# First attention layer on features of the unnormed X, factors per token at its outputs, and moved pieces, waits and low halves in both attention layers

## The chip, the cores and the metric

The kernel runs on one core of a Trainium2 chip. The metric is the device time in microseconds (us) of one execution, the median of several runs. Five engines work side by side, each through its own instructions in program order, and meet through semaphores: TensorE (PE in the profile; PEld is its load of weights), VectorE (DVE), ScalarE (ACT), GpSimd (POOL) and SyncE (SP), which issues most DMAs. PE writes into eight PSUM banks, from which ACT and DVE evacuate to SBUF.

## The reference, cut to what matters

X has 512 tokens of width 1024. Two blocks run one after the other. The first ends with a mixture of experts and a norm of the whole block; the second has two layers of attention and FFN.

```
# first block, per layer: x = x + mixer(rms_norm(x, norm_mix_g)); x = x + hierarchical_moe(rms_norm(x, norm_ffn_g))
return rms_norm(x, norm_final_g)
# second block, per layer i
h = rmsnorm(x, ln1_g[i]) @ w_in[i]
(fq, fk, fv, ff, dq, dk, dv, c_q, c_kv, k_r) = jnp.split(h, split_points, axis=-1)
o_fox = fox_group(fq, fk, fv, ff, fgate_b[i])            # bias from cumsum of log_sigmoid(ff + b)
o_diff = diff_group(dq, dk, dv, lq1, lk1, lq2, lk2, diff_norm_g[i], lam_init)   # ends in rmsnorm(o, norm_g)
o_mla = mla_group(c_q, c_kv, k_r, q_norm_g[i], w_uq[i], kv_norm_g[i], w_ukv[i], pos)
x = x + jnp.concatenate([o_fox, o_diff, o_mla], axis=-1) @ w_o[i]
up = causal_dwconv(rmsnorm(x, ln2_g[i]) @ w_up[i], conv_w[i], conv_b[i])
x = x + (silu(up[:F]) * up[F:]) @ w_down[i]
```

A norm is a factor per token times a gain per channel: (x * r[token] * g[channel]) @ W = r[token] * ((x * g[channel]) @ W). Between the two blocks two norms follow one another: `norm_final_g` on X itself, and `ln1_g[0]` on its result.

## The kernel before

**Stages.** In order of time: a first mixer and its experts to about 668 us, a recurrent mixer and its experts to about 1314 us, the middle norm, attention 1 (1320 to 1600), FFN 1 (to 1965), attention 2 (1965 to 2240, the same rows as attention 1, 642.7 us later) and FFN 2. X (four chunks `c` of 128 tokens) stays in SBUF.

**Dense weights.** Every dense product is a sum of three matmuls of reduced-precision operands: high part of the features by high part of the weights, low by high, high by low. A weight arrives by a DMA that SP issues into one of four raw slots, in units of two halves (4 x 128 rows, up to 512 columns). ACT writes the high part of a half (`W.hi`, L275), and DVE or POOL the low part (`W.lo`, L283: a `tensor_tensor` of 128x1024 or 128x512). In `Weights.add` the halves are numbered in program order; even halves have their low part on DVE, odd ones on POOL. There are six split buffers, so a half is split up to six halves ahead of its use. Within an attention layer halves 0 to 3 belong to the product `mla`, 4 to 7 to `dq`, 8 to 11 to `dk`, 12 to 15 to `dv`, 16 to 19 to `fqk`, 20 to 23 to `fv` and 24 to 31 to the output product `atto` (24 to 27 for its first 512 columns, n = 0).

**Features.** The rows of X (after the norm, `XN`) are transposed by PE (L473, `tensor_half`), two chunks of tokens at a time; ACT writes the high part with the gain as a scale (L481), DVE the low part (L491). `tensor_first_product` (L556) starts the first product on the features of chunks 0 and 1 before those of 2 and 3 are there.

**The end of the experts.** `moe` adds the last expert's result to X by pieces (c, n) of 128 tokens and 512 columns: two matmuls (L1553, L1554) into a bank and one addition of DVE (L1776). All four pieces with n = 0 come ahead of those with n = 1. Behind them PE runs 18 matmuls whose result nobody reads (L408, `tensor_busy`), reads a register and branches on whether more slots of experts are needed (not in these runs).

**The middle norm.** `middle_norm` takes the sum of squares of each chunk (ACT L425, an activation with an accumulator, and its read), its root (L432), a reciprocal (DVE L440), and rescales X in place with `norm_final_g` (DVE L2712; the gain lies in raw slot 0, which becomes free for a next weight only when it was read last). The second norm does the same on that X and writes `XN` (DVE L460). Chunks 0 and 1 come first.

**Attention, PE's order.** Products `mla`, `dq`; transposes of the ranks (L529, wait `ckv`); the `up` products (L2161 and L2164, each group evacuated by ACT or DVE); the cumulated sums of the gates (L2170, wait `cum`); two of the four pieces of `dk` (L2132, 24 matmuls each); transposes of q1 and k1 (L529); and then a pipeline of score steps (L2089, `tensor_scores`; L2120, `tensor_values`) with the rest of `dk`, the products `dv`, `fqk` and `fv` between its steps. DVE applies the norm of the differential heads (L2497, 16 instructions of 128x128) while PE computes `fv`; the next things on DVE are low halves 24, 26 and 28, and then the maxima of the `fox` scores (L2386), for which ACT's exponentials (L2265) wait, and PE for those.

Of the kernel before, what the change touches and what calls it, by code (L numbers as in the profile page):

```python
# [11 lines left out]
ALU = mybir.AluOpType  # L12
ACT = mybir.ActivationFunctionType
AX = mybir.AxisListType.X

P = 128
# [20 lines left out]
TURN_BANKS, PIECE_BANK = (4, 5, 6), (7,)  # L37
# [5 lines left out]
    ("conv_b_2", 88), ("q_norm_g_2", 4), ("kv_norm_g_2", 2), ("norm_ffn_g", 16),  # L43
]
# [106 lines left out]
class Rows:  # L151
# [4 lines left out]
    def __init__(self, XN, before, hi, lo, gain):  # L156
        self.XN, self.before, self.hi, self.lo, self.gain = XN, before, hi, lo, gain
        self.H = (lambda k: hi[:, k, :], lambda k: lo[:, k, :])
        self.done = {}

# [11 lines left out]
class Weights:  # L172
# [23 lines left out]
    def add(self, key, parts, split=True, expert=False):  # L196
# [111 lines left out]
def program(nc, A, pack, const, out):  # L308
# [34 lines left out]
    junk = sb("junk", [P, D], BF16)  # L343

# [108 lines left out]

    def norm_of_rows(rows):
# [8 lines left out]
    def tensor_half(rows, half):  # L463

        rows.done[half] = []
        for j in range(KD // 2):
            bank = banks.take(bf)
            rows.done[half].append(len(bf.banks))
            for k in (2 * j, 2 * j + 1):
                for c in (2 * half, 2 * half + 1):  # L470
                    PE.wait_total(xn, rows.before + (c + 1 if c < NT - 1 else NT + k // (KD // 2)))
# [114 lines left out]
    def plan_cols(key, w, c0, n, order=(0, 1)):  # L586
        for u in order:
            W.add(key, [(4, n, w[512 * u:512 * u + 512, c0:c0 + n].rearrange("(k p) n -> p k n", p=P))])

    def plan_out(key, w, order=(0, 1)):  # L590
        for n in range(2):
            plan_cols((key, n), w, 512 * n, 512, order)
# [210 lines left out]
    lsg, lse = sig("log_sigmoid_in"), sig("log_sigmoid_exp")  # L803

# [572 lines left out]
    def moe(layer, last_square, last_norm, next_half, next_norm):  # L1377
# [178 lines left out]
        def tensor():  # L1556
# [64 lines left out]
        ahead = 2 if next_norm else NT  # L1621

        def scalar():
# [37 lines left out]
            scalar_squares(whole, range(ahead))  # L1661
# [124 lines left out]
        def vector():  # L1786
            vector_route()
            for p in range(PAIRS):
# [18 lines left out]
            for c in range(NT):  # L1807
                vector_combine(c, (0,))
            for c in range(NT):
                if next_norm and c == 3:  # L1810
                    vector_norm(next_norm, ((0, 1), (1, 1)))
                vector_combine(c, (1,))
# [36 lines left out]
        with nc.If(nblocks > 0):  # L1849
            with nc.Fori(0, nblocks):  # L1850
# [85 lines left out]
                for c in range(NT):  # L1936
# [9 lines left out]
                    act.wait_ge(s_loop, n[0])  # L1946
                    step(act.activation(junk[:, :], X[:, c, :], ACT.Square, accum_out=SM[:, c:c + 1]))
                    act.wait_ge(s_loop, n[0])
                    step(act.activation(SM[:, c:c + 1], SM[:, c:c + 1], ACT.Sqrt, bias=ONE[:, 2:3], scale=1.0 / D))
                    act.wait_ge(s_loop, n[0])  # L1950
# [892 lines left out]
```

## Time and profile of the kernel before

| what | value |
|---|---|
| time, median of 3 runs | 2614.44 us (2613.68 to 2616.26) |
| the profiled execution's own time | 2616.33 us |
| its span in the profile | 2615.1 us |
| granted TensorE clock, mean | 0.996 |
| PE busy | 2562.8 us, 98% of the span, 13324 matmuls |
| DVE / ACT / POOL busy | 1133.2 / 914.3 / 356.7 us |

The span begins with the first instruction and ends with the last. Starts are in us from the span's start. In a row of the timeline stand the start, the time from the first start to the last end, engine, line, operation, output <- input and count; in brackets the idle time before, and what ended it. The ends of matmuls are modelled, so neighbouring rows of PE overlap by some tenths. In a row by windows each engine has its busy time and, in parentheses, its instructions; behind them stand the granted clock as a share of 2.4 GHz (0.50 is 1.2 GHz), the busy share of the DMA engines and GB/s.

### The profile page before, as it was taken

What the parts mean: (1) busy time and instruction counts of PE and PEld (TensorE: products, weight loads), DVE (VectorE), ACT (ScalarE), POOL (GpSimd) and SP (SyncE); (2) the same over time, 40 slices, a digit from 0 to 9 for tenths busy, and PEclk for the clock granted to TensorE, in tenths of its full rate; (3) what the DMA queues carried; (4) which work ended last, traced back from release to release, by engine and by line L of the source; (5) the groups of instructions that cost most, each with busy time, mean ns of one, the idle gap of its engine ahead of it and who ended that gap; (6) DMA issues with size and microseconds to landing.
All of it is one profiled execution on the core that took longest, in us unless ns stands there. A gap on an engine that the chain in (4) does not pass through costs nothing.

```text
span 2615.1 us, 32699 instructions
## 1 busy us (share of the span) xinstructions
PE 2562.8 (98%) x13324; PEld 1789.3 (68%) x13324; DVE 1133.2 (43%) x1971; ACT 914.3 (35%) x1741; POOL 356.7 (14%) x160
## 2 busy tenths in 40 slices
PE   9999999999999999999989999999999999999999
PEld 7874444444777444445477778888888767888887
DVE  2543233323685233223353453552554344465264
ACT  4431111111484111111164454442345454443233
POOL 2200000000340000000030011231222002222212
PEclk9999999999999999999999999999999999999999
DMA  6248999999325999999921112232232112223222
GB/s 219 83 193 356 421 421 420 421 421 420 113 97 214 412 420 422 421 421 421 407 80 59 55 65 81 97 108 86 65 117 71 62 33 81 75 87 124 78 65 80
DMA packets 133367, 542.23 MB, mean 207 GB/s; under 512 B 13024, under 2 KB 24672, under 8 KB 84064
## 3 DMA queue, kind: packets, MB, share of 16 engines
q1 hardware_dynamic: 129264, 536.94, 52.5%
q10 hardware_dynamic: 3952, 3.17, 0.4%
q8 instruction: 108, 1.77, 0.3%
q14 instruction: 43, 0.35, 0.0%
HBM read 537.98 MB, written 2.10 MB: 207 GB/s over the span
## 4 chain that ended last, share of the span: by engine, by line
PE 91%; DVE 4%; DMA 2%; ACT 2%; issue 1%; POOL 0%; SPq 0%; POOLq 0%; DVEq 0%; ACTq 0%
PE ps L622 21%; PE ps L1516 16%; PE ps L624 15%; PE ps L1538 8%; PE ps L646 5%; PE ps L1492 4%; PE ps L555 4%; PE ps L2132 3%; PE ps L1553 2%; PE ps L1554 2%; DMA w<-in_moe_w_up 2%; PE ps L2089 2%; PE ps L2120 2%; PE ps L556 1%; PE ps L2111 1%
## 5 line engine op out<-in xcount | busy, mean ns | idle before, releaser
L283 POOL TENSOR_TENSOR w<-w,w 128x1024 fp32r<-128x1024 f32 (+2 forms) x136 | 335.2, 2474 | 2206.3 <-ACT w L275 2202.1
L622 PE MATMUL ps<-w,w 128*128 128x512 f32 x2592 | 590.7, 389 | 2.6 <-POOL w L283 2.6
L622 PEld LDWEIGHTS ps<-w,w 128*128 128x128 f32 x2592 | 486.1, 188 | 104.8 <-POOL w L283 3.4
L1516 PE MATMUL ps<-w,w 128*64 128x512 f32 x2048 | 445.4, 592 | 3.5 <-issue 2.0
L624 PE MATMUL ps<-w,w 128*128 128x512 f32 (+1 forms) x1872 | 408.8, 379 | 5.3 <-DVE w L541 3.0
L624 PEld LDWEIGHTS ps<-w,w 128*128 128x128 f32 x1872 | 337.9, 188 | 72.6 <-issue 5.9
L275 ACT ACTIVATE w<-w 128x1024 fp32r<-128x1024 f32 (+2 forms) x260 | 251.5, 999 | 348.9 <-PE ps L624 177.9
L283 DVE TENSOR_TENSOR w<-w,w 128x1024 fp32r<-128x1024 f32 (+2 forms) x124 | 200.8, 1626 | 350.6 <-ACT w L275 348.1
L1516 PEld LDWEIGHTS ps<-w,w 128*64 128x64 f32 x2048 | 149.0, 137 | 293.6 <-issue 293.6
L1538 PE MATMUL ps<-w,w 128*64 128x512 f32 x1024 | 226.8, 595 | 0.8 <-ACT w L1614 0.8
L1764 DVE TENSOR_TENSOR w<-ps,w 128x512 f32<-128x512 f32 x32 | 34.7, 1083 | 388.8 <-PE ps L1516 388.8
L1538 PEld LDWEIGHTS ps<-w,w 128*64 128x64 f32 x1024 | 70.7, 137 | 139.8 <-issue 138.8
L2634 DVE SCALAR_TENSOR_TENSOR w<-ps,PK,w 128x511 f32<-128x511 f32 (+1 forms) x176 | 131.8, 749 | 75.5 <-ACT w L2590 72.4
L1776 DVE TENSOR_TENSOR X<-ps,X 128x512 f32<-128x512 f32 x256 | 159.5, 679 | 1.1
L646 PE MATMUL ps<-w,w 128*128 128x512 f32 x528 | 122.6, 391 | 0.2 <-DVE X L724 0.2
L1492 PEld LDWEIGHTS ps<-w,w 128*128 128x128 f32 x896 | 111.0, 191 | 2.4
L646 PEld LDWEIGHTS ps<-w,w 128*128 128x128 f32 x528 | 98.5, 188 | 20.7 <-issue 0.6
L1492 PE MATMUL ps<-w,w 128*128 128x256 f32 x896 | 111.6, 282 | 0.0
L1553 PE MATMUL ps<-w,w 128*128 128x512 f32 x256 | 109.0, 426 | 0.0
L1658 ACT ACTIVATE w<-ps,w 128x512 fp32r<-128x512 f32 x64 | 44.0, 688 | 180.3 <-PE ps L1538 180.3
L1783 DVE SCALAR_TENSOR_TENSOR w<-ps,w,w 128x512 fp32r<-128x512 f32 x64 | 48.0, 751 | 133.8 <-ACT w L1658 133.8
L2132 PE MATMUL ps<-w,w 128*128 128x512 f32 x384 | 101.6, 411 | 0.0
(257 smaller groups left out, 2471.4 us busy)
## 6 DMA issues: line engine op xcount, KB each, us to landing
w<-in_moe_w_gate SPq DMA_DIRECT2D x128, 1024.0 KB, 15.6
w<-in_moe_w_up SPq DMA_DIRECT2D x128, 1024.0 KB, 18.5
w<-in_moe_w_down SPq DMA_DIRECT2D x128, 1024.0 KB, 15.0
w<-in_w_up SPq DMA_DIRECT2D x40, 1024.0 KB, 5.1
w<-in_w_down SPq DMA_DIRECT2D x20, 1024.0 KB, 5.2
w<-in_w_in SPq DMA_DIRECT2D x16, 1024.0 KB, 5.2
w<-in_ab_w_in SPq DMA_DIRECT2D x10, 1024.0 KB, 7.6
w<-in_c_w_in SPq DMA_DIRECT2D x8, 1024.0 KB, 7.8
```

Of the source, the lines that this page charges most:

```text
L275: up(self.whi, self.S.e.activation(hi, raw, ACT.Copy))
L283: up(self.wlo[self.low[s][0]], lane.e.tensor_tensor(lo, raw, hi.bitcast(F32), ALU.subtract))
L622: ins = pe.matmul(bank[:, :], wp[:, k, P * o:P * o + P], ap(k0 + k), start=first, stop=stop)
L624: ins = pe.matmul(bank[:, 0:width], ap(k0 + k)[:, P * o:P * o + P], wp[:, k, :], start=first, stop=stop)
L646: ins = pe.matmul(bank_of(o)[:, 0:width], ap(k)[:, P * o:P * o + P], wp, start=(k == 0 and pi == 0), stop=(hi is rows[-1][0] and pi == 2))
L1492: i = pe.matmul(bank[:, 256 * k:256 * k + 256], rows_part(part, c)[:, t:t + P], SELR[:, c, :], start=(part == 0 and c == 0), stop=(part == ...
L1516: ins = pe.matmul(bank[64 * e:64 * e + 64, :], XG[p % 3][:, 4 * u + k, 64 * e:64 * e + 64], w[e][:, k, :], start=(u == 0 and k == 0), stop ...
L1538: ins = pe.matmul(two[n][64 * e:64 * e + 64, :], HDT[:, 2 * u + k, 64 * e:64 * e + 64], w[e][:, k, 512 * n:512 * n + 512], start=(u == 0 a ...
L1553: pe.matmul(bank[:, :], s_, YH[:, 512 * n:512 * n + 512], start=True, stop=False)
L1776: up(bx.free, dve.tensor_tensor(x, bank[:, :], x, ALU.add))
L2132: ins = pe.matmul(bank[:, :], wp, ap(k), start=(k == 0 and pi == 0), stop=(k == KD - 1 and pi == 2))
L2634: ins = dve.scalar_tensor_tensor(y[:, d:T], bank[:, 0:T - d], col("conv_w_2", 132 * i + 44 * tap + f), y[:, d:T], ALU.mult, ALU.add)
```

## The change

1. **End of the second experts.** The last pieces go (0,0), (1,0), (0,1), (1,1), then the same for chunks 2 and 3. The 18 dummy matmuls are gone, and so are the squares and roots that stood there. DVE computes the product of both gains once, early.
2. **Raw features in attention 1.** PE transposes X itself as soon as chunks 0 and 1 are added, runs six dummy matmuls, and begins the products. Both norms are worked out behind the features (`scalar_behind`, `vector_behind`): X is still rescaled in place, and the product of both factors of each token is `TOKEN_SCALE`. Where tokens are partitions (`CM`, `LF`, `KR`, `DV`, `FV`), ACT's evacuations apply it as a scale. Where tokens are columns, it is needed as a row `TR` 128x512: DVE multiplies the identity by the factors, PE adds up with a matrix of ones (one fp32 matmul inside `dq`), DVE copies; POOL multiplies 12 tiles of 128x512 (`DQ`, `DK`, `FQK`) by it, before PE's scores that read them (wait `spread`). All this is in attention 1 alone.
3. **Both attentions.** Half of the first `dk` piece (k = 0 to 3) stands ahead of the `up` products, two rows of the third piece stand ahead of the waits for the first scores, and the waits for the evacuated `dv` and `fv` stand in `tensor_values` in place of behind the products.
4. **Both attentions.** Low halves 24 to 27 (`atto`, n = 0) are all POOL's; 24 and 26 were DVE's.

```diff
-                engine = int(s % 2 == 1 or s < self.ring_start + NSPLIT)
+                engine = int(pool or s % 2 == 1 or s < self.ring_start + NSPLIT)
...
-        plan_out(("atto", i), A["w_o_2"][i], OUT_ORDER)
+        plan_out(("atto", i), A["w_o_2"][i], OUT_ORDER, pool=True)
...
                 for c in (2 * half, 2 * half + 1):
+                    if rows.raw:
+                        PE.wait_total(bx.free, rows.raw[c])
...
-            for n in range(2):
-                for c in range(NT):
-                    tensor_combine(PAIRS - 1, c, (n,))
-            tensor_busy(10 if next_norm else 18)
+            for c, n in last_pieces:
+                tensor_combine(PAIRS - 1, c, (n,))
+            if next_norm:
+                tensor_busy(10)
...
+            last_pieces = [(c, n) for two in ((0, 1), (2, 3)) for n in range(2) for c in two]
...
-            scalar_squares(whole, range(ahead))
+            if next_norm:
+                scalar_squares(whole, (0, 1))
...
         def tensor_scores(m, two):
+            if rows.raw and two[0][1] != "mla":
+                h = two[-1][2]
+                PE.wait_ge(spread, 4 + h + 1 if two[0][1] != "fox" else 8 + 2 + h // 2 * 2)
...
         def tensor_values(m, two):
+            if two[0][1] != "mla":
+                PE.wait_ge(ba.free, 10 + 8 + 4 + 1 + (4 if two[0][1] == "diff0" else 8))
...
         def tensor():
+            if rows.raw:
+                tensor_half(rows, 0)
+                tensor_busy(6)
             tensor_first_product(rows, ("mla", i), 1, 420, ba)
-            tensor_product(("dq", i), ALL4, 512, H, ba, feature=True)
+            def token_row(n):
+                if n == 1:
+                    PE.wait_ge(diagonal, 1)
+                    bank = banks.take(brow)
+                    up(brow.full, pe.matmul(bank[:, :], cst("ones"), TR[:, :], start=True, stop=True))
+            tensor_product(("dq", i), ALL4, 512, H, ba, feature=True, between=token_row if rows.raw else None)
             PE.wait_ge(ckv, 8)
             tensor_features(lambda c, k: CM[:, c, P * k:P * k + P], 3, lambda k: bv if k % 2 else ba)
+            piece, first_keys = tensor_pieces(("dk", i)), banks.take(bpc, PIECE_BANK)
+            banks.among = UP_BANKS
+            piece(0, range(KD // 2), first_keys)
...
-            piece = tensor_pieces(("dk", i))
-            for o in (0, 1):
-                piece(o, range(KD), banks.take(bpc))
+            piece(0, range(KD // 2, KD), first_keys)
+            piece(1, range(KD), banks.take(bpc))
...
-            PE.wait_ge(ba.free, 10 + 8 + 4)
-            PE.wait_ge(bv.free, 2 + 4)
...
-                if p < DIFF_STEP:
+                if p < DIFF_STEP and p:
...
             PE.wait_ge(bpc.free, 2)
+            piece_rows(piece, 2, range(2))
+            PE.wait_ge(ba.free, 10 + 8 + 4)
+            PE.wait_ge(bv.free, 2 + 4)
...
+            rows.behind[0]()
...
             def cm_evacuate():
+                if rows.raw:
+                    S.wait_ge(token_scale, 1)
...
+                    up(ss, act.activation(CM[:, c, :], bank[:, 0:384], func, **of_token(c)))
...
+            if rows.raw:
+                G.wait_ge(brow.free, 1)
+                for o in range(4):
+                    scale_tokens(ba.free, 4 + o + 1, DQ[:, o, :])
+                for o in range(4):
+                    scale_tokens(bpc.free, o + 1, DK[:, o, :])
+            for key in (("dk", i), ("dv", i)):
+                gpsimd_product(key)
+            if rows.raw:
+                for n, o in enumerate((0, 2, 1, 3)):
+                    scale_tokens(bpc.free, 4 + n + 1, FQK[:, o, :])
...
+        def scalar_behind():
+            first_squares((2, 3))
+            for c in range(NT):
+                S.wait_total(xw, written + c + 1)
+                square(X[:, c, :], D, TOKEN_SCALE[:, c:c + 1])
+                scalar_roots(96 + c, 1, D)
+
+        def vector_behind():
+            update((2, 3))
+            W.raw_consumed_at[unit.n] = (xw, xw.n)
+            for c in range(NT):
+                vector_roots(96 + c, 1, roots + NT + c + 1)
+            V.wait_total(token_scale, up(token_scale, dve.tensor_tensor(TOKEN_SCALE, TOKEN_SCALE, SM[:, 0:NT], ALU.mult)))
+            for c in range(NT):
+                ins = dve.tensor_scalar(TR[:, P * c:P * c + P], ident, TOKEN_SCALE[:, c:c + 1], None, ALU.mult)
+            up(diagonal, ins)
```

What that moves on the engines, first for PE in attention 1, between the transposes of the ranks and the pieces of `dk`. In the kernel before (L529 are the transposes, L2161 and L2164 the `up` products, L2170 the sums, L2132 the pieces):

```order
L529 MATMUL ps<-CT,w_22528_11253 128x128 [waits s_bank_act_free]
L529 MATMUL ps<-CT,w_22528_11253 128x128 x3
L2161 MATMUL ps<-w_26624_50,w_12288_11247 128x384 [waits s_bank_dve_free,s_bank_act_free,s_raw1]
L2161 MATMUL ps<-w_26624_50,w_12288_11247 128x384
L2164 MATMUL ps<-w_26624_50,w_12288_11247 128x512
```

and in the changed kernel, where L2153 is the piece, L2194 and L2197 the `up` products:

```order
L2153 MATMUL ps<-w_0_74,w_34816_63 128x512
L2153 MATMUL ps<-w_4096_75,w_34816_63 128x512
L2153 MATMUL ps<-w_0_74,w_35840_69 128x512
L2194 MATMUL ps<-w_26624_50,w_12288_11147 128x384 [waits s_bank_dve_free,s_bank_act_free,s_raw1]
L2194 MATMUL ps<-w_26624_50,w_12288_11147 128x384
L2197 MATMUL ps<-w_26624_50,w_12288_11147 128x512
```

Twelve matmuls of the first `dk` piece (its last three are shown) now stand between the transposes of the ranks and the wait for their evacuation.

Second, DVE behind the norm of the differential heads in attention 1, before:

```order
L2497 SCALAR_TENSOR_TENSOR w_8192_11244<-w_8192_11244,SM,dnB 128x128 [waits s_dve_step]
L2497 SCALAR_TENSOR_TENSOR w_8192_11244<-w_8192_11244,SM,dnB 128x128 x15
L283 TENSOR_TENSOR w_41984_72<-w_28672_51,w_40960_66 128x1024 [waits s_whi]
L283 TENSOR_TENSOR w_33792_68<-w_30720_52,w_32768_62 128x1024 [waits s_whi]
L283 TENSOR_TENSOR w_37888_70<-w_24576_49,w_36864_64 128x1024 [waits s_whi]
L2386 TENSOR_REDUCE AT<-ps 128x1 [waits s_scores_full] x2
```

and in the changed kernel:

```order
L443 RECIPROCAL SM<-SM 128x16 [waits s_root]
L2547 SCALAR_TENSOR_TENSOR w_8192_11144<-w_8192_11144,SM,dnB 128x128 [waits s_dve_step]
L2547 SCALAR_TENSOR_TENSOR w_8192_11144<-w_8192_11144,SM,dnB 128x128 x15
L285 TENSOR_TENSOR w_37888_70<-w_24576_49,w_36864_64 128x1024 [waits s_whi]
L2430 TENSOR_REDUCE AT<-ps 128x1 [waits s_scores_full] x2
```

Two low halves of 128x1024 are gone between the norm and the maxima.

Third, POOL in the same place (halves 21, 23, 25, 27 and 29), before:

```order
L283 TENSOR_TENSOR w_35840_69<-w_24576_49,w_34816_63 128x512 [waits s_whi]
L283 TENSOR_TENSOR w_39936_71<-w_26624_50,w_38912_65 128x512 [waits s_whi]
L283 TENSOR_TENSOR w_44032_73<-w_28672_51,w_43008_67 128x1024 [waits s_whi]
L283 TENSOR_TENSOR w_35840_69<-w_30720_52,w_34816_63 128x1024 [waits s_whi]
L283 TENSOR_TENSOR w_39936_71<-w_24576_49,w_38912_65 128x1024 [waits s_whi]
```

and in the changed kernel (L2577 are the multiplications of `FQK` by the token row):

```order
L2577 TENSOR_TENSOR w_20480_11157<-w_20480_11157,TR 128x512 [waits s_pieces_free] x4
L285 TENSOR_TENSOR w_39936_71<-w_26624_50,w_38912_65 128x512 [waits s_whi]
L285 TENSOR_TENSOR w_41984_72<-w_28672_51,w_40960_66 128x1024 [waits s_whi]
L285 TENSOR_TENSOR w_44032_73<-w_28672_51,w_43008_67 128x1024 [waits s_whi]
L285 TENSOR_TENSOR w_33792_68<-w_30720_52,w_32768_62 128x1024 [waits s_whi]
L285 TENSOR_TENSOR w_35840_69<-w_30720_52,w_34816_63 128x1024 [waits s_whi]
L285 TENSOR_TENSOR w_39936_71<-w_24576_49,w_38912_65 128x1024 [waits s_whi]
```

POOL has two more low halves in a row, five of 128x1024 where there were three.

## Rows read from the trace of the kernel before

**Rows 1.** Page: busy time, share and instructions of TensorE

```profile
PE 2562.8 (98%) x13324; PEld 1789.3 (68%) x13324; DVE 1133.2 (43%) x1971; ACT 914.3 (35%) x1741; POOL 356.7 (14%) x160
```

**Rows 2.** Waits of PE: line, awaited engine and line: total us, times, longest

```profile
PE ps L473 <- DVE w L460: 8.5, 4, 5.5
...
PE ps L2161 <- ACT w L701: 3.0, 2, 1.5
...
PE ps L2089 <- ACT w L701: 2.3, 4, 0.7
...
PE ps L529 <- ACT w L2275: 1.8, 2, 1.1
PE ps L2089 <- DVE w L2488: 1.7, 2, 0.9
```

**Rows 3.** Timeline of PE: end of the experts, middle norm, first products

```profile
1310.58 4.06 PE L408 MATMUL ps<-CT 128*128 128x512 bf16 x18
1320.14 0.45 PE L473 MATMUL ps<-CT,w 128*128 128x128 f32 x1 [5.50 <-DVE w L460]
1321.42 3.25 PE L473 MATMUL ps<-CT,w 128*128 128x128 f32 x15 [0.83 <-DVE w L460]
1325.04 4.86 PE L556 MATMUL ps<-w,w 128*128 128x420 f32 x24 [0.37 <-issue]
...
1345.43 4.94 PE L622 MATMUL ps<-w,w 128*128 128x512 f32 x21
```

**Rows 4.** Timeline of DVE and then ACT: last additions, a square of the middle

```profile
1307.69 0.75 DVE L1783 SCALAR_TENSOR_TENSOR w<-ps,w,w 128x512 fp32r<-128x512 f32 x1 [0.94 <-ACT w L1658]
1308.36 4.86 DVE L1776 TENSOR_TENSOR X<-ps,X 128x512 f32<-128x512 f32 x8
...
1327.69 1.04 ACT L425 ACTIVATE junk<-X 128x1024 bf16<-128x1024 f32 x1
```

**Rows 5.** Timeline at the first experts' end: ACT's features, PE's first product

```profile
671.51 3.04 ACT L481 ACTIVATE w<-ps,PK 128x256 fp32r<-128x256 f32 x8 [1.62 <-PE ps L473]
...
673.46 5.99 PE L555 MATMUL ps<-w,w 128*128 128x256 f32 x48 [0.68 <-POOL w L283]
```

**Rows 6.** Timeline of ACT: a load of its function table and the activation behind

```profile
1400.64 1.28 ACT L2265 ACT_TABLE_LOAD   x1 [3.15 <-DVE AT L2386]
1401.94 0.69 ACT L2265 ACTIVATE w<-ps,AT 128x512 f32<-128x512 f32 x1
```

**Rows 7.** By windows of 2 us: busy time and count, clock, DMA share

```profile
1318.00:1320.00 2.00, 0.00 (x0) 0.00 (x0) 0.92 (x2) 1.97 (x5) 0.00 (x0) 0.50 0.01 4
...
1382.00:1384.00 2.00, 2.00 (x7) 1.53 (x7) 1.86 (x12) 0.00 (x0) 0.00 (x0) 0.58 1.05 408
```

**Rows 8.** Timeline of PE: an fp32 product and the pieces of `dk`

```profile
1371.58 1.02 PE L2164 MATMUL ps<-w,w 128*128 128x512 f32 x2
...
1381.04 12.78 PE L2132 MATMUL ps<-w,w 128*128 128x512 f32 x48
```

**Rows 9.** Timeline of DVE beside `fv` in attention 1

```profile
1522.14 9.44 DVE L2497 SCALAR_TENSOR_TENSOR w<-w,SM,dnB 128x128 f32<-128x128 f32 x16
1531.51 3.49 DVE L283 TENSOR_TENSOR w<-w,w 128x1024 fp32r<-128x1024 f32 x3
1534.91 0.48 DVE L2386 TENSOR_REDUCE AT<-ps 128x1 f32<-128x128 f32 x2
```

**Rows 10.** DVE line L2497 alone: count, minimum, median and maximum in ns

```profile
L2497 DVE SCALAR_TENSOR_TENSOR w<-w,SM,dnB x32: 339/341/2564, 1522.1 to 2173.9; 128x128 f32<-128x128 f32 x32
```

**Rows 11.** Timeline of POOL beside `fv` in attention 1

```profile
1521.82 1.30 POOL L283 TENSOR_TENSOR w<-w,w 128x512 fp32r<-128x512 f32 x1 [61.80 <-ACT w L275]
1523.72 4.83 POOL L283 TENSOR_TENSOR w<-w,w 128x1024 fp32r<-128x1024 f32 x2 [0.60 <-ACT w L275]
```

**Rows 12.** Timeline of PE: first wait of the `fox` steps

```profile
1537.90 1.06 PE L529 MATMUL ps<-CT,w 128*128 128x128 f32 x8 [1.10 <-ACT w L2275]
```

**Rows 13.** Page: DMA issues of attention weights, KB each, median us to landing

```profile
w<-in_w_in SPq DMA_DIRECT2D x16, 1024.0 KB, 5.2
```

More of the change, by code:

```diff
@@ L43 @@
     ("conv_b_2", 88), ("q_norm_g_2", 4), ("kv_norm_g_2", 2), ("norm_ffn_g", 16),
+    ("norm_final_g", 8),
 ]
@@ L159, in __init__ @@
         self.done = {}
+        self.raw, self.behind = None, (lambda: None, lambda: None)
 class Unit:
@@ L452, in rows_at, with raw_rows @@
         return Rows(XN, (NT + 1) * mark["norms"], *HT_[place], gain)
+    def raw_rows(place, gain):
+        return Rows(X, None, *HT_[place], gain)
     def norm_of_rows(rows):
@@ L470, in tensor_half @@
                 for c in (2 * half, 2 * half + 1):
-                    PE.wait_total(xn, rows.before + (c + 1 if c < NT - 1 else NT + k // (KD // 2)))
+                    if rows.raw:
+                        PE.wait_total(bx.free, rows.raw[c])
+                    else:
+                        PE.wait_total(xn, rows.before + (c + 1 if c < NT - 1 else NT + k // (KD // 2)))
                     t = 2 * P * (k % 2) + P * (c % 2)
@@ L803, in program @@
     lsg, lse = sig("log_sigmoid_in"), sig("log_sigmoid_exp")
+    gains, token_scale, diagonal, spread = (sig(n) for n in ("gains", "token_scale", "diagonal", "spread"))
+    brow = handoff("token_row")
     def sync_start():
@@ L1620, in whole @@
             S.wait_total(bx.free, added + 8 * (PAIRS - 1) + NT + c + 1)
-        ahead = 2 if next_norm else NT
+        last_pieces = [(c, n) for n in range(2) for c in range(NT)]
+        if not next_norm:
+            last_pieces = [(c, n) for two in ((0, 1), (2, 3)) for n in range(2) for c in two]
         def scalar():
@@ L1787, in vector @@
             vector_route()
+            if not next_norm:
+                both = cols("norm_final_g", 0, KD)
+                up(gains, dve.tensor_tensor(both, both, cols("ln1_g_2", 0, KD), ALU.mult))
             for p in range(PAIRS):
@@ L1806, in vector @@
                 vector_rest(p)
[L1807 to L1810, printed above, removed]
+            for c, n in last_pieces:
+                if next_norm and (c, n) == (3, 1):
                     vector_norm(next_norm, ((0, 1), (1, 1)))
-                vector_combine(c, (1,))
+                vector_combine(c, (n,))
         def gpsimd():
@@ L2430, in vector @@
         def vector():
+            if rows.raw:
+                V.wait_total(gains, 1)
             vector_rows(rows, last_norm, late, ahead)
+            rows.behind[1]()
             vector_product(("mla", i))
@@ L2450, in vector, with token_row @@
             up(cum, dve.tensor_copy(sb_cum[:, 0:16], sb_cum[:, 16:32]))
-            vector_product(("dq", i))
+            def token_row():
+                bank = brow.next(V)
+                up(brow.free, dve.tensor_copy(TR[:, :], bank[:, :]))
+            vector_product(("dq", i), token_row if rows.raw else None)
             bank = bv.next(V)
```

88 lines of the change are left out of this document (50 added, 38 removed).

## The prediction, made before the changed kernel ran

> **What bounds the kernel now.** The page comes first: PE is busy 98% of the span [rows 1], so the time is PE's program plus its gaps, and work taken off another engine pays only where PE waited for it. The view of PE's waits names the gaps in the changed places [rows 2]: the transposes behind the middle norm waited 8.5 us over the whole run, 5.5 of them at once; the `up` products 3.0 in two waits; scores behind an evacuation 2.3 in four waits (the longest, 0.7, once in each attention at `dv`, the rest at `fv`); scores behind a feature 1.7 in two; the `fox` transposes 1.8 in two. The timelines then show what stood on the other engines in each gap, and the windows the granted clock, since a gap costs twice where the clock falls behind it: 0.50 after the gap of the middle norm, 1.2 GHz, with PE idle before, and 0.58 in the `dk` pieces [rows 7].
>
> **The middle norm.** Before, the last addition's matmuls end about 1310.7; 18 dummies follow to 1314.6, PE waits until 1320.14, 15 more transposes take 3.25 us at the low clock, and the first product starts at 1325.04 [rows 3]. DVE's eight last additions take 4.86 us, 0.61 each, from 1308.36 [rows 4]. In the new order chunks 0 and 1 are the first four of them: 1308.36 + 4 x 0.61 = 1310.8. But the pieces with n = 1 now come early and wait for L1783, whose second instruction ends at 1307.69 + 0.75 = 1308.44 [rows 4]; that moves PE's last piece to about 1311.4. Transposes of raw X start at 1311.7. A first bank is full some five transposes later, 0.55 at full clock (half of 3.25/15 each [rows 3]), and ACT, which arrives fresh behind a branch, loads its table, 1.28 [rows 6]: features from about 1313.7. Where the first experts end, the product began 673.46 - 671.51 = 1.95 behind the first feature [rows 5]. So it starts at 1315.6, **9.4 us earlier**. The ends: 8.4 if the branch costs PE a microsecond more, 9.8 if it costs less, 10.7 if the table is loaded in cover. All later work of PE moves with it.
>
> The Trainium skill, page ScalarE: Activation LUTs, section What ACT_TABLE_LOAD costs, adds to such a load a drain of about 1.4 us, 2.66 in all. In the trace the activation behind the load starts 1.30 after the load's start [rows 6], so no drain is seen behind it; by the page the gain would be about 8.0.
>
> **The factors.** Squares, roots and updates of X now run under the products. A square takes about 1.4 us of ACT with its read and root (1.04 of it is in [rows 4]), eight of them 11, under `mla` and `dq` (20 us of PE each; `mla` from 1325.04 to 1345.43 [rows 3]). The token row costs PE one fp32 matmul of 128x512, half of the pair in [rows 8]: about 0.5 at its pitch, 1.0 with the change of operands and the wait for its bank, **+1.0** (0.5 to 1.5). The scales at ACT's evacuations cost nothing: the same instructions. POOL's twelve multiplications of 128x512 take as long as a low half of that size, 1.30 [rows 11]. They must be done before scores that PE reaches 10 us and more later for `DQ` and `DK`; for `FQK` the last of them is done only half a microsecond ahead of PE, by my count. I take 0; the ends are 0 and one multiplication, +1.3.
>
> **Pieces and waits, both attentions.** Twelve matmuls of `dk` (2.7 us) now lie between the transposes of the ranks and the `up` products, whose wait was 1.5 each time [rows 2]. In attention 2 it goes whole, **-1.5**. In attention 1 the factors make the evacuations late (ACT's queue holds squares, and the gates' logarithm follows), so I take only **-0.6** (0 to -1.5). The two rows of the third piece ahead of the first scores cover the feature wait of 0.87 each: **-1.6** [rows 2]. The `dv` waits of 0.7 go, since another bank's values are computed meanwhile: **-1.3** (0 to -1.4). The `fv` waits, some 0.45 each, are swallowed by what DVE does there, below: 0.
>
> **The clock of the pieces.** 48 matmuls of `dk` took 12.78 [rows 8]. At the pitch of `dq`'s 21 in 4.94, (4.94 - 0.39)/20 = 0.2275, they would take 11.1. So 1.7 were lost in each attention while the clock stood at 0.58 [rows 7], right behind the 20 short matmuls of the sums. Half a piece less follows them in the changed kernel, but they stay. I take 0 for the likeliest case; the other end is -3.4, and is a rival.
>
> **Low halves moved to POOL.** This is the term that decides. Beside `fv`, DVE ran 16 norm instructions in 9.44 us, though the shortest takes 339 ns [rows 9, 10]; the longest took 2564 ns, as long as a POOL low half of 128x1024, 4.83/2 = 2.4 [rows 10, 11]. The pattern is that under a POOL instruction with two SBUF inputs one such DVE instruction starts and ends with it: three or four are held until POOL pauses at 1523.72 + 4.83 = 1528.55, and the other 11 follow at 0.26 each, to 1531.5. Three low halves to 1535.0 and the maxima at 1534.91 follow [rows 9], then ACT's table and exponentials, for which PE waited 1.10 until 1537.90 [rows 12].
>
> With the change POOL has 23 (1.3) and then 24, 25, 26, 27, 29 in one row: its inputs are ready, so it runs from 1523.7 for 5 x 2.4 = 12 us, until about 1535.5, without the pause in which DVE did its 11. Five or six norm instructions pass meanwhile, ten follow at 0.26 to 1538.1, one low half (3.49/3 = 1.16, ends overlapping) to 1539.1. The maxima come at 1539.1 instead of 1534.9: +4.15, and the row [rows 12] shows no slack in that chain. Twice: **+8.3**. The ends: -1.8, if DVE isn't held and the two halves it lost make the chain early, and +12, if the last norm waits for half 29's neighbour as well. PE then stands idle 5.2 us at a place, as long as in the middle norm, where the clock fell to 0.50 behind it [rows 3, 7]; there 15 transposes and a few matmuls cost some 1 to 2 us more. I take 1 each: **+2.0** (0 to 4).
>
> The Trainium skill, page SBUF — State Buffer, section Who interferes with whom, speaks against this part: a DVE instruction with two SBUF inputs contends with a GpSimd one that reads SBUF, and whoever issues first holds the shared pair for its whole instruction. The trace agrees by its 2564 ns under POOL's 2.4 us. Were the rule not to hold here, the sum would lack the last two terms and come to -15.
>
> **The sum.** -9.4 + 1.0 - 0.6 - 1.5 - 1.6 - 1.3 + 8.3 + 2.0 = -3.1. The profiled execution took 2616.33 (1.2 outside its span), so it would take 2613.2. The median of the runs lies 1.9 below it: **2611.3**.
>
> **Rivals.**
> *A, the sum above*: 2611.3, its own range 2607 to 2616 by the bounds of the middle, the row and the idle clock.
> *B, POOL does not hold DVE long.* If POOL pauses between its halves (ACT's high part 29 comes late, or DVE wins the turn more often), DVE saves 2 x 1.16 = 2.3 and the `fox` wait falls by 1.1 and 0.7. For it: POOL did pause before, 0.60 ahead of its first long half [rows 11]. Against: the high parts were written while POOL ran. Sum -9.4 + 1.0 - 2.1 - 1.6 - 1.3 - 1.8 = -15.2: 2614.4 - 15.2 = 2599.2.
> *C, A with the pieces at full clock.* The short matmuls are followed by fewer matmuls of `dk`, and PE has no wait ahead of the `up` products, so the clock may stay: a further -3.4, 2607.9. Against: the fall came behind the short matmuls, which remain.
> *D, the factors come late; slower than before.* The norm's gains lie in raw slot 0 until the updates of chunks 2 and 3, which now stand behind the features, at about 1332.8 by my count of ACT's queue. The second unit of `dq` needs that slot, lands 5.2 later alone [rows 13], at 1338, and up to 1343 with three more units behind it; split by 1347 it is needed at 1336 + 11 = 1347. It costs nothing up to a landing at 1343, and one for one beyond. With each microsecond of delay `CM`, `ckv` and the token row move too, since `cm_evacuate` waits for all eight squares. If release comes 4 later, PE loses 4 there, 2 at the ranks, and 2 by the clock: 2611.3 + 8 = 2619.3, and 2622 at most. Against: in the first 20 us ACT has little else.
> *E, the middle does not shorten*, because ACT is the last there by some queue of high parts: the gain is 5, and the time 2615.5. It ends as the same.
>
> **How the numbers follow.** A 0.42, B 0.20, C 0.14, D 0.14, E 0.05, others 0.05. A measurement of this kernel can tell about 0.2%, 5.2 us, from no change, so faster is below 2609.2 and slower above 2619.7. Faster: B, C and a fifth of A, 0.20 + 0.13 + 0.08 and 0.02 of the others, 0.43. Slower: half of D and some others, 0.10. Same: the rest, 0.47. The range of 8 in 10 leaves out what lies under B's middle and the upper part of D: 2598 to 2618. Since both A and B have weight, A's own range of 2607 to 2616 stands beside it.
>
> **What would show each step.** In the changed profile: the first product (L566) starts at about 1315.6 and its transposes at 1311.7; behind them windows at full clock. An idle PE before `up` (L2194) in attention 2 of 0, and none before the first scores. POOL's low halves beside `fv` as one row of six, DVE's L2547 x16 taking 15 to 16 us instead of 9.44, and PE waiting 5 us for ACT in front of the `fox` transposes. If L2547 takes 10 us or less, B is right. If `dq` has a gap of microseconds for a low half, or the ranks' transposes wait, D is. The prediction is wrong above all if POOL's turn comes otherwise than in this row, or if the late maxima find slack on PE.

## The result, and the profile after

The changed kernel is **slower**: 2622.09 us (median of 16 runs, 2618.63 to 2624.0) against 2614.93 (16 runs), a ratio of 1.0027 with a 95% interval of 1.0021 to 1.0034. The prediction was 2611.3 with a range of 2598 to 2618. The profiled execution took 2621.18 us with a span of 2619.9; that of before took 2616.33, so the two profiles differ by 4.85 and the medians by 7.2: the profile of before lies 1.4 above the median of its 16 runs, that of the changed kernel 0.9 below.

The busy times of the changed kernel's page, and then its waits of PE (line, awaited engine and line: total us, times, longest), to be laid beside [rows 1, 2]:

```profile
PE 2564.6 (98%) x13314; PEld 1793.2 (68%) x13314; DVE 1142.6 (44%) x1969; ACT 917.3 (35%) x1743; POOL 375.5 (14%) x176
```

```profile
PE ps L2141 <- DVE w L2468: 8.6, 2, 4.6
PE ps L632 <- ACT w L711: 6.8, 1, 6.8
...
PE ps L483 <- DVE w L467: 3.4, 4, 1.2
```

The 5.5 us before the transposes (L473, now L483) are gone, and so are the waits of L2161, L2089 and most of L529. Two new waits head the list: 6.8 us at once in a product (L632) for ACT, and 8.6 in two waits of the value products (L2141) for DVE.

Where PE stood at the same places of the program, from the starts in both timelines of PE:

| PE begins | before | after | moved since the row above |
|---|---|---|---|
| first product of attention 1 | 1325.04 | 1315.68 | -9.4 |
| `dq` | 1345.43 | 1342.96 | +6.9 |
| transposes of the ranks | 1367.22 | 1367.09 | +2.3 |
| `fv` | 1517.53 | 1513.66 | -3.7 |
| first product of FFN 1 | 1602.51 | 1607.28 | +8.6 |
| `fv` of attention 2 | 2160.20 | 2160.45 | -4.5 |
| first product of FFN 2 | 2245.27 | 2250.13 | +4.6 |

Three stretches gain 17.6 us together and four lose 22.5. The starts of two profiles can't be compared to a tenth: at DVE's last additions, ahead of the changed place, the changed kernel already runs 0.39 later (1308.75 against 1308.36).

The losses have two causes. The timeline of PE at the first one:

```profile
1311.76 1.91 PE L483 MATMUL ps<-CT,X 128*128 128x128 f32 x16
1313.51 1.46 PE L411 MATMUL ps<-CT 128*128 128x512 bf16 x6
1315.68 4.86 PE L566 MATMUL ps<-w,w 128*128 128x420 f32 x24 [0.72 <-issue]
...
1342.96 7.28 PE L632 MATMUL ps<-w,w 128*128 128x512 f32 x25 [6.80 <-ACT w L711]
```

The transposes now start at 1311.76 and take 1.91 for 16, where [rows 3] had 3.25 for 15. Then `dq` waits 6.80 for ACT, and its first 25 matmuls take 7.28, where 21 took 4.94 before. On ACT, at the same time (L277 writes high parts, L2353, L2354 and L711 evacuate `mla`):

```profile
1336.53 2.00 ACT L277 ACTIVATE w<-w 128x1024 fp32r<-128x1024 f32 x2 [1.96 <-DMA w<-in_w_in]
1340.96 1.06 ACT L277 ACTIVATE w<-w 128x1024 fp32r<-128x1024 f32 x1 [2.42 <-DMA w<-in_w_in]
1341.92 0.56 ACT L2353 ACTIVATE w<-ps,SM 128x384 f32<-128x384 f32 x1
1342.38 0.25 ACT L2354 ACTIVATE sb_cum<-ps,SM 128x4 f32<-128x4 f32 x1
1342.53 0.29 ACT L711 ACTIVATE w<-ps,SM 128x32 f32<-128x32 f32 x1
```

and on the queue of SP (a row that spans its wait for the slot), where the third load starts about 1331.4 and the others follow at once:

```profile
1299.33 32.41 SPq L261 DMA_DIRECT2D w<-in_w_in  x3
1331.85 0.44 SPq L261 DMA_DIRECT2D w<-in_w_uq  x1
```

The factors themselves were ready by 1335. `mla` was finished by 1336.2. But in ACT's program high parts 6, 7 and 8 stand ahead of the evacuation of `mla`; part 8 is the first of `dk`, and its weights, behind three other loads in the queue, landed at 1340.9. The first bank of `dq` is one that `mla` holds until that evacuation.

The second loss, in the timelines of DVE, POOL and PE beside and behind `fv`, against [rows 9, 11, 12]:

```profile
1518.28 15.70 DVE L2547 SCALAR_TENSOR_TENSOR w<-w,SM,dnB 128x128 f32<-128x128 f32 x16
1533.91 1.21 DVE L285 TENSOR_TENSOR w<-w,w 128x1024 fp32r<-128x1024 f32 x1
1535.04 0.48 DVE L2430 TENSOR_REDUCE AT<-ps 128x1 f32<-128x128 f32 x2
```

```profile
1517.96 13.25 POOL L285 TENSOR_TENSOR w<-w,w 128x512 fp32r<-128x512 f32 x6 [1.38 <-ACT w L277]
```

```profile
1535.83 1.97 PE L2141 MATMUL ps<-w,w 128*128 128x64 f32 x8 [4.62 <-DVE w L2468]
1538.03 1.94 PE L539 MATMUL ps<-CT,w 128*128 128x128 f32 x8 [0.23 <-ACT w L2307]
```

Six halves in one row without a pause, the norm in 15.70 us instead of 9.44, PE idle 4.62, and behind it matmuls at about half speed: 1.94 for the eight transposes that took 1.06 [rows 12]. By windows of 2 us (columns as in [rows 7]):

```profile
1538.00:1540.00 2.00, 1.98 (x10) 1.67 (x10) 0.12 (x1) 2.00 (x6) 0.00 (x0) 0.50 0.87 336
1544.00:1546.00 2.00, 2.00 (x12) 1.96 (x11) 0.28 (x1) 0.46 (x1) 0.00 (x0) 0.50 0.00 0
```

A second low stretch follows in this stage. The second group of 48 matmuls of `atto` (n = 0) takes 12.73 in attention 1 and 11.16 in attention 2, behind the same wait (in the kernel before 11.16 and 11.13):

```profile
1571.19 12.73 PE L634 MATMUL ps<-w,w 128*128 128x512 f32 x48 [1.14 <-DVE w L551]
2215.60 11.16 PE L634 MATMUL ps<-w,w 128*128 128x512 f32 x48 [1.14 <-DVE w L551]
```

### The profile page after: what moved, and what is told of

The parts are those of the page before. It is cut to its first block, busy times and chain, and to the rows that moved or that the text cites. A ratio compares the mean times of both kernels' runs of the same rounds, so it can differ in the third digit from the quotient of the medians.

```text
span 2619.9 us, 32705 instructions
## 1 busy us (share of the span) xinstructions
PE 2564.6 (98%) x13314; PEld 1793.2 (68%) x13314; DVE 1142.6 (44%) x1969; ACT 917.3 (35%) x1743; POOL 375.5 (14%) x176
## 4 chain that ended last, share of the span: by engine, by line
PE 90%; DVE 4%; DMA 2%; ACT 2%; issue 1%; POOL 0%; SPq 0%; ACTq 0%; POOLq 0%; DVEq 0%
PE ps L632 21%; PE ps L1528 16%; PE ps L634 15%; PE ps L1550 8%; PE ps L656 5%; PE ps L1504 4%; PE ps L565 4%; PE ps L2153 3%; PE ps L1565 2%; PE ps L1566 2%; PE ps L2108 2%; DMA w<-in_moe_w_up 2%; PE ps L2141 2%; DVE w L2547 1%; PE ps L2130 1%
## 5 line engine op out<-in xcount | busy, mean ns | idle before, releaser
L632 PE MATMUL ps<-w,w 128*128 128x512 f32 x2592 | 592.8, 390 | 9.4 <-ACT w L711 6.8
L632 PEld LDWEIGHTS ps<-w,w 128*128 128x128 f32 x2592 | 487.2, 188 | 112.6 <-issue 8.6
L277 ACT ACTIVATE w<-w 128x1024 fp32r<-128x1024 f32 (+2 forms) x260 | 251.5, 999 | 349.1 <-PE ps L634 179.5
L1798 DVE SCALAR_TENSOR_TENSOR w<-ps,w,w 128x512 fp32r<-128x512 f32 x64 | 48.1, 751 | 133.6 <-ACT w L1672 133.6
```

Of the source, the lines that this page charges most:

```text
L277: up(self.whi, self.S.e.activation(hi, raw, ACT.Copy))
L632: ins = pe.matmul(bank[:, :], wp[:, k, P * o:P * o + P], ap(k0 + k), start=first, stop=stop)
```

## The experiments

Twelve kernels, each in five rounds beside the kernel before. The table has the medians, with that of before in the same job in parentheses, and the ratio with its 95% interval. Where a kernel is set beside the changed one, its 2622.09 is of another job; the kernel before differed by at most 0.5 us between the jobs.

| kernel | what it is | us | ratio |
|---|---|---|---|
| half_dve | changed, part 4 undone | 2610.72 (2614.46) | 0.9981 [0.9972, 0.9990] |
| evac_first | changed, `mla` evacuated earlier | 2619.45 (2614.46) | 1.0018 [1.0009, 1.0028] |
| pool_after_norm | changed, POOL waits for the norm | 2605.78 (2614.46) | 0.9965 [0.9951, 0.9978] |
| before_pool | before, part 4 alone | 2626.27 (2614.46) | 1.0048 [1.0034, 1.0062] |
| before_pieces | before, part 3 alone | 2609.40 (2614.76) | 0.9983 [0.9974, 0.9992] |
| factors_alone | before, parts 1 and 2 | 2616.30 (2614.76) | 1.0006 [0.9997, 1.0015] |
| gains_slot2 | changed, gains in another slot | 2615.41 (2614.76) | 1.0004 [0.9995, 1.0013] |
| evac_log_norm | three reorderings together | 2595.79 (2614.76) | 0.9932 [0.9918, 0.9945] |
| pool_after_8 | POOL waits for half the norm | 2605.76 (2614.70) | 0.9966 [0.9954, 0.9979] |
| before_pool_wait | before, part 4 and POOL's wait | 2610.64 (2614.70) | 0.9985 [0.9976, 0.9994] |
| evac_log | changed, two of the reorderings | 2613.05 (2614.70) | 0.9993 [0.9984, 1.0002] |
| evac_log_half | evac_log, part 4 undone | 2601.61 (2614.70) | 0.9949 [0.9935, 0.9962] |

**The parts one by one** add up. Parts 1 and 2 alone: +1.5, an interval that holds 0. Part 3 alone: -5.4. Part 4 alone: +11.8. The sum is +8.0, and the changed kernel is +7.2 above its kernel before.

**Part 4, undone and alone.** half_dve:

```diff
-        plan_out(("atto", i), A["w_o_2"][i], OUT_ORDER, pool=True)
+        plan_out(("atto", i), A["w_o_2"][i], OUT_ORDER)
```

> The changed kernel with part 4 undone: low halves 24 and 26 are DVE's again in both attentions. Theory (POOL's six halves in a row hold DVE's norm of the differential heads, DVE's maxima come late, PE stands idle 4.6 us and then runs on the low clock): both fox stages get shorter by about 8.6 us each, 17 together, so about 2605 where the changed kernel takes 2622. The norm's 16 instructions take 9 to 10 us instead of 15.7. Rival (the stage grew because of the moved waits of dv and fv, or because PE arrives there 4 us earlier against an unchanged DVE): less than 5 us are gained and the idle time before the fox transposes stays.

11.4 below the changed kernel, not 17: the 17 took the 8.6 of attention 1 for both stages, where attention 2 had lost 4.6. The norm takes 9.43 us again, as expected, and the 4.6 us before the value products shrink to 0.63. But the stage keeps part of its low clock in attention 1 (0.50 from 1536 to 1544). The timeline of PE in half_dve:

```profile
1531.80 1.10 PE L2141 MATMUL ps<-w,w 128*128 128x64 f32 x8 [0.63 <-DVE w L2468]
1534.00 1.07 PE L539 MATMUL ps<-CT,w 128*128 128x128 f32 x8 [1.09 <-ACT w L2307]
...
1539.55 1.91 PE L539 MATMUL ps<-CT,w 128*128 128x128 f32 x8
```

Two waits of 0.63 and 1.09 stand here behind one another, where the kernel before had only the one of 1.10 [rows 12] and kept its clock. But the pair alone doesn't explain the fall. before_pieces, below, has the same pair (0.64 and 1.09) and evac_log_half too (0.65 and 1.10), and the clock of both stays at 1.00. The timeline of PE in before_pieces:

```profile
1533.58 1.10 PE L2122 MATMUL ps<-w,w 128*128 128x64 f32 x8 [0.64 <-DVE w L2428]
1535.78 1.07 PE L529 MATMUL ps<-CT,w 128*128 128x128 f32 x8 [1.09 <-ACT w L2279]
...
1540.08 1.04 PE L529 MATMUL ps<-CT,w 128*128 128x128 f32 x8
```

before_pool is the mirror: `pool=True` handed through `plan_out`, `plan_cols` and `add` in the kernel before.

> The kernel before with part 4 alone: low halves 24 to 27 on POOL in both attentions. Theory: +8 us in each attention, about 2614.9 + 16 = 2631. Rival (part 4 hurts only together with the earlier arrival of PE): within 4 us of the kernel before.

+11.8, 4 less than the 16 expected. The rival that part 4 hurts only beside the other parts falls. In before_pool the timelines of DVE and PE show the same picture as in the changed kernel:

```profile
1518.97 15.70 DVE L2497 SCALAR_TENSOR_TENSOR w<-w,SM,dnB 128x128 f32<-128x128 f32 x16
```

```profile
1536.52 1.97 PE L2120 MATMUL ps<-w,w 128*128 128x64 f32 x8 [4.09 <-DVE w L2424]
```

**Is it the held norm, or the amount of POOL's work?** pool_after_norm keeps all six halves on POOL and only delays them:

```diff
-            for key in (("fqk", i), ("fv", i)):
-                gpsimd_product(key)
+            for s, _, _ in W.steps(("fqk", i)) + W.steps(("fv", i)):
+                if s + SPLITS == W.steps((("atto", i), 0))[0][0]:
+                    G.wait_ge(o_done, 4 * NT)
+                W.lo(s + SPLITS, G)
```

> The changed kernel, but POOL waits before low half 24 until DVE has finished its norm of the differential heads; POOL keeps all its halves. Theory of the held norm: the norm takes about 5 to 6 us instead of 15.7, the maxima are no longer late, and the time falls by 17 to 19 us, to about 2604. Rival (it is the amount of POOL's work that makes something late: the halves themselves, or their order on the queue): the time stays or rises, since POOL now starts later with the same work.

16.3 below the changed kernel, near the 17 to 19 expected. The timelines of DVE and POOL:

```profile
1519.26 5.07 DVE L2547 SCALAR_TENSOR_TENSOR w<-w,SM,dnB 128x128 f32<-128x128 f32 x16
1525.26 2.64 DVE L285 TENSOR_TENSOR w<-w,w 128x1024 fp32r<-128x1024 f32 x1 [0.92 <-ACT w L277]
1527.82 0.47 DVE L2430 TENSOR_REDUCE AT<-ps 128x1 f32<-128x128 f32 x2
```

```profile
1524.41 12.63 POOL L285 TENSOR_TENSOR w<-w,w 128x1024 fp32r<-128x1024 f32 x5 [4.17 <-DVE w L2547]
```

The norm takes 5.07, the maxima come at 1527.8 in place of 1535.0, and PE waits for neither. The same five halves of POOL, held back 4.17 us, cost PE nothing, though one low half of DVE beside them takes 2.64 instead of 1.21.

pool_after_8 has `2 * NT` in place of `4 * NT` in that wait: POOL may begin when 8 of the 16 are done.

> As pool_after_norm, but POOL begins low half 24 when 8 of the 16 norm instructions are done and not all 16. Theory (one DVE instruction passes for each POOL instruction while POOL has no pause): POOL begins its five halves about 3 us after the norm's start and runs 12 us on end; five instructions are held through it and three follow, so the norm still takes about 15 us, the maxima are as late as in the changed kernel, and the time is 2620 to 2622. Rival (DVE is slowed in proportion to the overlap): half of pool_after_norm's gain, 2614.

2605.76: the whole gain of pool_after_norm (2605.78). Both the theory's number and the rival's miss. The timelines of POOL and DVE:

```profile
1522.19 14.55 POOL L285 TENSOR_TENSOR w<-w,w 128x1024 fp32r<-128x1024 f32 x5 [2.06 <-DVE w L2547]
```

```profile
1519.15 5.06 DVE L2547 SCALAR_TENSOR_TENSOR w<-w,SM,dnB 128x128 f32<-128x128 f32 x16
```

POOL was released at 1522.19 in the midst of the norm, and this time it was POOL that stood: its five instructions span 14.55 us, not 12.63, because the first takes 4.30 where it took 2.41, and DVE's 16 took as long as without POOL. "One DVE instruction passes for each of POOL's" is thus only what happens when POOL has begun first. When DVE's row is under way, the row runs to its end. The Trainium skill, page SBUF — State Buffer, section Who interferes with whom, says that issue order decides who blocks. Both cases are here. What its wording does not tell is how rows of instructions fare: with DVE under way, its eight remaining back-to-back instructions all ran before POOL's; with POOL first, one DVE instruction passed with each of POOL's.

before_pool_wait is the kernel before with part 4 and this wait.

> The kernel before with part 4 and the wait of pool_after_norm. Theory (the move of the halves is worth something once DVE isn't held): the fox waits of 1.10 and 0.73 and some of the clock go, 1.5 to 4 below the kernel before, about 2612. Rival (POOL, starting late with five halves, makes a later half late): at or above the kernel before.

-4.1: with its order mended, part 4 gains.

**The wait of `dq`.** evac_first:

```diff
-            scalar_product(("mla", i), cm_evacuate)
+            if rows.raw:
+                cm_evacuate()
+            scalar_product(("mla", i), None if rows.raw else cm_evacuate)
```

> The changed kernel with one thing moved: in attention 1, ACT evacuates the product mla before the high parts 6, 7 and 8 and not behind them. Theory (PE's dq waited 6.8 us for a bank of mla, whose evacuation stood on ACT behind a high part that waited for its weights): dq starts about 6 us earlier and the low clock behind the gap goes, together -7.6 us, about 2614.5. Rival (the weights themselves are what PE needs): dq stops a few matmuls later for its own low half, and less than 2 us are gained.

The wait is gone, `dq` starts at 1334.42 (this profile runs 1.7 us ahead of the changed kernel's already at its first product), and yet only 2.6 of 7.6 us are gained. The timeline of PE, then that of DVE (L806 belongs to the logarithm of the gates, L2505 is the second evacuation of the ranks), shows the next one:

```profile
1358.51 3.01 PE L2153 MATMUL ps<-w,w 128*128 128x512 f32 x12
1365.62 2.90 PE L2194 MATMUL ps<-w,w 128*128 128x384 f32 x4 [4.11 <-DVE w L2505]
```

```profile
1359.15 2.38 DVE L806 TENSOR_SCALAR sb_cum<-sb_cum 128x16 f32<-128x16 f32 x1
...
1361.87 2.35 DVE L285 TENSOR_TENSOR w<-w,w 128x1024 fp32r<-128x1024 f32 x2
1364.13 0.68 DVE L2502 COPY TR<-ps 128x512 f32<-128x512 f32 x1
1364.74 0.74 DVE L2505 TENSOR_SCALAR w<-ps,PK 128x512 f32<-128x512 f32 x1
```

PE's four matmuls behind this gap take 2.90 instead of 1.45: the wait moved on by one stage and took its low clock with it. About 2.2 us of the gap are again a hold: L806 takes 2.38 where its neighbours take 0.17, while POOL writes a low half (1359.10, 2.41).

gains_slot2 attacks the loads: the gains of the norm are planned behind `mla`'s two units, and so lie in the slot that only `dk`'s first unit needs.

```diff
+        if i == 0:
+            plan_middle()
         plan_cols(("dq", i), w, 772, 512)
...
-    plan_middle()
     for i in range(2):
         plan_att(i)
```

> The changed kernel with the gains of the middle norm in the third raw slot, loaded behind mla's two units, so that dq's second unit no longer waits for their release and only dk's first does. Theory (the release of the slot at about 1331 lets four loads start at once, the last of them makes ACT's high part 8 late, and mla's evacuation stands behind it): high part 8 comes about 3.5 us earlier, PE's wait before dq falls from 6.9 to about 3.5 and the clock behind it falls less, so 2 to 5 less than the changed kernel, unless the logarithm chain takes it as in evac_first (then 1 to 2 less). Rival (the evacuation waits for the factors, not for the loads): no change of the wait.

-6.7 against the changed kernel. PE's timeline, then ACT's: the high parts follow the last root at once, three in a row, and the wait is 2.21.

```profile
1338.49 12.77 PE L632 MATMUL ps<-w,w 128*128 128x512 f32 x48 [2.21 <-ACT w L711]
```

```profile
1334.61 2.94 ACT L277 ACTIVATE w<-w 128x1024 fp32r<-128x1024 f32 x3
```

So the held slot and the order on ACT make the wait together, and the rival that the evacuation waited for the factors falls. That this run gained more than was expected, and more than the larger advance of evac_first, has a reason in the two timelines: counted from the first product of each profile, `dq` starts 2.2 us later than in evac_first and the transposes of the ranks 3.8 us later, and the `up` products come without a gap.

**Parts 1 and 2, and part 3.** factors_alone is the changed kernel with parts 3 and 4 undone; before_pieces has part 3 in the kernel before.

> The changed kernel with parts 3 and 4 undone, so the experts' end and the factors alone. Theory: the 9.4 us won in the middle norm are given back by dq's wait for its bank (6.9), the low clock behind it (1.6) and the token row (0.5), so within 1.5 us of the kernel before, about 2614.5. Rival (the factors also make the ranks late where no piece of dk stands ahead of the up products): 2 to 4 us above the kernel before.

> The kernel before with part 3 alone (pieces and waits moved) in both attentions. Theory: per attention the wait before the up products (1.5), the feature wait (0.9, of which a later wait of 0.6 takes some back), the dv wait (0.7) and the low clock of the dk pieces (1.7) go, 4.2 together, so 8.4 less in all, about 2606. Rival (earlier arrival at the fox stage only lengthens the low clock there, as in half_dve): 3 to 5 less, about 2610.

factors_alone: the 9.4 us are given back whole, the waits of 6.9 before `dq` and of 1.5 before the `up` products are there; +1.5, at the edge of the theory, below the rival's 2, and not told apart from no change. before_pieces: -5.4, between the theory's 8.4 and the rival's 3 to 5. Its waits before `up`, before the first scores and at `dv` are gone, and of the two low stretches of the clock behind the sums one is left, in attention 1 (0.66 from 1384 to 1388).

**Putting it together.** evac_log_norm has evac_first and pool_after_norm, and DVE's logarithm moved behind the second evacuation of the ranks:

```diff
-            log_sigmoid(sb_cum[:, 16:32], sb_cum[:, 0:16], z[0], z[1], z[2])
-            up(cum, dve.tensor_copy(sb_cum[:, 0:16], sb_cum[:, 16:32]))
...
             up(bv.free, dve.tensor_scalar(CTT[:, 1, :], bank[:, :], ckv_gain(1), None, ALU.mult))
+            log_sigmoid(sb_cum[:, 16:32], sb_cum[:, 0:16], z[0], z[1], z[2])
+            up(cum, dve.tensor_copy(sb_cum[:, 0:16], sb_cum[:, 16:32]))
```

> Three reorderings on the changed kernel, no work changed: mla evacuated before the high parts 6 to 8 (as in evac_first), DVE's logarithm of the gates behind the second evacuation of the ranks (it stood ahead of it, and PE waited 4.1 us for that in evac_first), and POOL's halves from 24 on behind the norm (as in pool_after_norm). Theory: the 9.4 us of the middle are kept, so 7 to 8 less than pool_after_norm's 2605.8: 2598. Rival (a third thing is late behind these two, the sums of the gates or the token row): 2601 to 2604.

**2595.79**, 19.0 below the kernel before and 26.3 below the changed one, with no instruction added or dropped but a wait, and 2 us better than expected. PE's timeline has no gap from the first product to the pieces:

```profile
1334.31 11.21 PE L632 MATMUL ps<-w,w 128*128 128x512 f32 x48
...
1361.22 1.45 PE L2194 MATMUL ps<-w,w 128*128 128x384 f32 x4
```

> The changed kernel with mla's early evacuation and DVE's logarithm moved, part 4 as it stands. Theory (the two troubles are independent): 16 above evac_log_norm's 2595.8, as between the changed kernel and pool_after_norm: 2612, so 10 below the changed kernel.

> As evac_log, with part 4 undone (halves 24 and 26 on DVE again). Theory: half_dve's 2610.7 less 10, about 2600.5; the rest to 2595.8 is what part 4 is worth when POOL waits for the norm. If it comes to 2596, part 4 is worth nothing.

evac_log: 9.0 below the changed kernel, where 10 were expected, so the two troubles add up as independent ones do, within the noise. evac_log_half comes to 2601.6; part 4 with POOL's wait is worth the 5.8 from there to 2595.8.

## Why the prediction was wrong

By its steps, each against the stretch of the table of PE's starts:

- **The middle norm, -9.4.** The steps came as told: transposes at 1311.76 (forecast 1311.7), first product at 1315.68 (1315.6), the wait for L1798 0.47, the table load seen as counted. That it is right to a tenth is in part luck: counted from DVE's last additions, which began 0.39 later here, the gain is 9.7.
- **The factors, +1.0.** This is the step that failed: +9.2 in place of +1.0. The +1.0 was the price of the token row, and that was right: from the start of `dq` to the transposes of the ranks are 22.86 us in evac_first (1334.42 to 1357.28), at full clock, against 21.79 before (1345.43 to 1367.22). The failure is the price of nothing for squares, roots and updates that "run under the products": a wait of 6.8 and about 1.3 by the clock behind it. Rival D named the held slot and the loads behind it, and its count of the release (1332.8) was 1.4 us late. But it looked for the harm at `dq`'s second unit, and set the point from which it decides at a landing of 1343. The bank of `mla` was never asked after: ACT's program has a high part of `dk` ahead of the evacuation, and `dq`'s first bank behind it, so the limit was the end of `mla`, 1336, and the last load at 1340.9 was already past it. The low clock behind shows in the first 25 matmuls: 7.28, where the pitch of 0.2275 gives 5.85. gains_slot2 and evac_first show the two halves of the cause.
- **Pieces and waits.** Attention 2 was forecast at -3.0 and attention 1 at -2.1; measured up to `fv`: -4.5 and -3.7. The waits fell as said, less 0.57 for a new wait of scores for ACT in each; the rest is rival C, the low clock of the pieces: 36 of them take 8.47, at the full pitch, in both attentions. How much of that is the change's is open. In the profile of before the 48 pieces ran low in both attentions, but in three other profiles without part 3 (before_pool, before_pool_wait, factors_alone) the same 48 take 11.14 to 11.16, full pitch, in four of six cases. With part 3 all but one of 20 ran at full pitch, the one in before_pieces. So part 3 is likely to make the low stretch rarer, but C's price of 3.4 holds only against an execution that had it twice.
- **Low halves to POOL, +8.3 and +2.0.** The mechanism was right: one row of six, the norm in 15.70 (forecast 15 to 16), maxima 4.0 us late against the `fv` product before them (forecast 4.15). The whole, 10.3, is near before_pool's +11.8 and below pool_after_norm's 16.3, which also takes away waits that were there before. That it is near is in part luck, since both terms are mis-sized, in opposite directions. PE's idle time from `fv` to the FFN grew by 2.4 us in attention 1 and 2.2 in attention 2, not by 4.15 each: the chain had slack after all, because waits of 1.10 [rows 12], 0.47 and others were swallowed by the new one. The clock cost the rest of the 8.6 and 4.6, about 6.3 and 2.4, not 1 each. Of the 6.3, 1.6 are the second stretch (12.73 for 48 matmuls), which factors_alone has too (12.75), with part 4 undone. The prediction says of the rule on the shared pair that it "speaks against this part"; it is what the part rests on, and without the last two terms its sum is -13.4, not -15.
- **Rival B** falls: POOL made no pause. **Rival D** had the sign and the held slot right, with 0.14, and the wrong place. Its 2619.3, with 2622 at most, is near the result, but for another sum.

The sum in the profiled frame: forecast -3.1, measured +4.9. Of the 8.0 between, the factors are +8.2, the fox stages +2.9 (idle -3.7, clock +6.7), and the pieces -3.3; the rest is rounding.

Not settled is what makes the clock stay or fall at small gaps. The same pair of waits (0.63 and 1.09, 0.64 and 1.09) went with a fall in half_dve and with none in before_pieces, and behind the same wait of 1.14 the 48 matmuls of `atto` took about 12.7 in 10 of the 28 cases of the 14 profiles and about 11.15 in the others. So a term of some 1.6 us at such a place can come or go between two executions, and a difference of that size between two profiles is not by itself an effect of the change. The low stretch behind the long gap isn't fixed either: in attention 1 it lasted until about 1547 in the changed kernel and 1541 in before_pool, behind gaps of 4.62 and 4.09.

## What to carry to other kernels

When a stage is made to start earlier, list for the next two products not only what they read but which PSUM banks they take, and what stands ahead of those banks' evacuation in its engine's program; a prefetch that waits for a DMA there stops the main path. And when work is moved to GpSimd beside a row of VectorE instructions with two SBUF inputs, it is the order of the first instructions that decides: over both layers the same instructions made the kernel 16 us slower when they began ahead of VectorE's row than when they began in its midst or behind it. A gain of one step is to be read again behind each fix: here three reorderings together won 26 us, of which the first alone won 2.6.

## What the runs showed of the hardware

- GpSimd's `tensor_tensor` of 128x1024 began in the midst of 16 back-to-back VectorE instructions with two SBUF inputs and was held until their end: five of them spanned 14.55 us instead of 12.63, with VectorE's 16 unchanged at 5.06. In the other order VectorE's 16 took 15.70, five of them about 2.5 each, one with each GpSimd instruction, and GpSimd's were unchanged.
- TensorE's granted clock fell to 0.50 (1.2 GHz) behind 6.8 us, 4.6 us and 4.1 us without a matmul. It fell behind waits of 0.63 and 1.09 us in a stretch of short matmuls in one profile, and stayed at 1.00 behind 0.64 and 1.09 in another. The low clock cost about 1.3 us behind the gap of 6.8, in a stretch of matmuls of 128x512, and about 4.7 us behind the gap of 4.6, among the short matmuls of the fox stage.
